# Stick-breaking attention weights from two sigmoids and a running product, longest rows first

## What is computed

```python
for i in range(s_len // 128):                       # rows lo..hi of the queries
    z = einsum('bthd,bshd->bhts', q[:, lo:hi], k[:, :hi]) * 64 ** -0.5
    mask = (lo + arange(128))[:, None] > arange(hi)[None, :]
    log_keep = where(mask, log_sigmoid(-z), 0.0)
    after = cumsum(log_keep, axis=3, reverse=True) - log_keep
    log_a = where(mask, log_sigmoid(z) + after, -inf)
    outs.append(einsum('bhts,bshd->bthd', exp(log_a), v[:, :hi]))
y = (o * silu(z_gate)) @ out_w
```

## Time and profile before

| | us |
|---|---|
| median of 3 runs | 1669.52 |
| profiled execution | 1669.38 |
| its span | 1667.6 |
| TensorE busy | 1577.1 (95%) |
| VectorE busy | 965.4 (58%) |
| ScalarE busy | 712.1 (43%) |

### The profile page before, as it was taken

The page is one execution under the profiler, slowest core; times in us unless marked ns, Lnnn a source line. Parts: engine busy times, 40 slices in busy tenths (PEclk is TensorE's granted clock), DMA queues, the critical chain, the costliest instruction groups (busy, mean ns, idle before and its releaser), DMA issues. The chain is left out here.

```text
span 1667.6 us, 19671 instructions
## 1 busy us (share of the span) xinstructions
PE 1577.1 (95%) x7998; PEld 1246.6 (75%) x7998; DVE 965.4 (58%) x1202; ACT 712.1 (43%) x997; POOL 112.1 (7%) x77
## 2 busy tenths in 40 slices
PE   6999999889899899889999999999999999999998
PEld 3777777667689665568787786668787888878877
DVE  3669888796774677755347626654444444432353
ACT  4555666563432567754212354532332222232241
POOL 0000000023200000004000000000020000000120
PEclk7999999999999999999999999999999999999999
DMA  7434333323572110102221112112222222232243
GB/s 306 154 128 152 126 130 136 138 64 152 202 303 102 51 51 29 48 33 106 93 75 46 58 51 90 66 73 87 90 76 101 101 93 86 100 113 89 97 155 114
DMA packets 47386, 177.76 MB, mean 107 GB/s; under 512 B 3616, under 2 KB 20256, under 8 KB 31680
## 3 DMA queue, kind: packets, MB, share of 16 engines
q1 hardware_dynamic: 30368, 167.44, 27.2%
q10 hardware_dynamic: 16928, 9.06, 2.1%
HBM read 172.23 MB, written 4.26 MB: 106 GB/s over the span
## 5 line engine op out<-in xcount | busy, mean ns | idle before, releaser
L636 PE MATMUL bank<-HH,whi 128*128 128x512 f32 x1352 | 560.7, 415 | 26.2 <-issue 10.3
L638 PE MATMUL bank<-HH,wlo 128*128 128x512 f32 x1352 | 533.4, 395 | 0.0
L637 PE MATMUL bank<-HL,whi 128*128 128x512 f32 x1352 | 533.4, 395 | 0.0
L636 PEld LDWEIGHTS bank<-HH,whi 128*128 128x128 f32 x1352 | 257.6, 191 | 112.2 <-issue 57.6
L1138 DVE TENSOR_TENSOR wlo<-raw,whi 128x2048 fp32r<-128x2048 f32 (+2 forms) x118 | 267.3, 2265 | 88.4 <-ACT whi L1805 84.9
L638 PEld LDWEIGHTS bank<-HH,wlo 128*128 128x128 f32 x1352 | 257.4, 190 | 55.9
L637 PEld LDWEIGHTS bank<-HL,whi 128*128 128x128 f32 x1352 | 258.1, 191 | 48.2 <-issue 3.1
L1805 ACT ACTIVATE whi<-raw 128x2048 fp32r<-128x2048 f32 (+2 forms) x118 | 222.3, 1884 | 117.0 <-PE bank L638 116.0
L2354 POOL TENSOR_TENSOR SR<-SR,tmp 128x512 f32<-128x512 f32 x30 | 55.1, 1835 | 614.5 <-ACT tmp L1822 613.6
L666 PE MATMUL bank<-whi,HH 128*128 128x256 f32 x256 | 74.3, 290 | 0.0
L667 PE MATMUL bank<-whi,HL 128*128 128x256 f32 x256 | 72.4, 283 | 0.0
(11 more groups left out here) (312 smaller groups left out, 2235.2 us busy)
## 6 DMA issues: line engine op xcount, KB each, us to landing
raw<-wstream SPq DMA_DIRECT2D x113, 1024.0 KB, 4.8
aslot<-tstream SPq DMA_DIRECT2D x24, 512.0 KB, 3.3
A<-astream SPq DMA_DIRECT2D x8, 1024.0 KB, 18.2
AC<-scratch ACTq DMA_DIRECT2D x16, 512.0 KB, 5.9
QT<-tstream SPq DMA_DIRECT2D x12, 512.0 KB, 5.2
OZ<-tstream SPq DMA_DIRECT2D x12, 512.0 KB, 7.4
raw<-wstream SPq DMA_DIRECT2D x4, 768.0 KB, 4.2
X<-xT SPq DMA_DIRECT2D x1, 2048.0 KB, 8.2
```

What stands on the lines that cost most here:

```text
L636: e.matmul(o, wh[:, k, c], hi[:, kb0 + k, :], start=first and k == 0, stop=False)
L637: e.matmul(o, wh[:, k, c], lo[:, kb0 + k, :], start=False, stop=False)
L638: x = e.matmul(o, wl[:, k, c], hi[:, kb0 + k, :], start=False, stop=last and k == kb - 1)
```

## The change

The scores are no longer clamped and masked. ScalarE reads `zz` twice and writes sigmoid(-z) into `keeps` and sigmoid(z) into `att`. VectorE scans `keeps` in place from the last column to the second: state = state x keep + diag. `diag` is 0 except for a unit matrix in the last 128 columns, so the state is 0 beyond the diagonal, becomes 1 on it, and is the running product after it. The weights are `att` times `keeps` shifted by one column; the column behind the last is set to 0 once. There is no exponential or logarithm left. Rounds hold fewer steps (37 rounds in place of 38, transposes of row r-2 and products of row r-3 in round r), `zz` is freed by `s_bk` from ScalarE, and a pair of heads begins with its row of four key blocks. ScalarE loads the sigmoid's table once before the `k` projection and the Exp and Ln table after the attention; the eight loads around Tanh are taken out. The diff, without the list of semaphore names and a renamed wait:

```diff
@@ -78,7 +78,7 @@
...
        ("m_norm_g", 16), ("kv_ada_b", 16), ("kv_norm_g", 8), ("final_g", 8), ("mix_g", 8),
        ("lb", 4), ("onorm", 1), ("qn", 1), ("kn", 1), ("ffn_g", 8), ("ple_g", 8), ("dtb", 1), ("alog", 1)]
-CON = [("ident", 128), ("ones", 128), ("bones", 128), ("cmask", 128), ("bmask", 512)]
+CON = [("ident", 128), ("ones", 128), ("bones", 128), ("cmask", 128), ("diag", 512)]
 
 
...
@@ -314,7 +314,7 @@
...
     ccol = lambda name: cc[:, COFF[name][0]:COFF[name][0] + COFF[name][1]]
     ident, ones, bones = ccol("ident"), ccol("ones"), ccol("bones")
-    cmask, bmask = ccol("cmask"), ccol("bmask")
+    cmask, diag = ccol("cmask"), ccol("diag")
     one = lambda name, k: cv[:, VOFF[name][0] + k:VOFF[name][0] + k + 1]
     eps_ap, eps2_ap = eps[:, 0:1], eps[:, 1:2]
...
@@ -430,8 +429,12 @@
...
 
 
-    att = lambda a, hi: W[:, 2 * (a % 5):2 * (a % 5) + 2, 0:hi]
-    att_z = lambda a, hi: (W[:, 10:12, 0:hi], W[:, 12:14, 0:hi], SR[:, :, 0:hi])[a % 3]
+
+    rows_of = lambda a: 3 - a % 4
+    width = lambda a: 128 * (rows_of(a) + 1)
+    att = lambda a, hi: W[:, 2 * (a % 4):2 * (a % 4) + 2, 0:hi]
+    keeps = flat(W[:, 8:14, :])[:, 0:4 * (S + 1)].rearrange("p (a s) -> p a s", a=4)
+    keep = lambda a, c0, c1: keeps[:, 2 * (a % 2):2 * (a % 2) + 2, c0:c1]
     live = lambda *units: [a for a in units if 0 <= a < 32]
 
...
@@ -826,21 +829,21 @@
...
 
         def attention():
-            for r in range(-1, 37):
-                for a in live(r - 4):
-                    w.wait_ge(s_ax, a + 1)
+            for r in range(-1, 36):
+                for a in live(r - 2):
+                    w.wait_ge(s_ls, a + 1)
                     w.wait_ge(s_at, a)
                     for j in range(2):
-                        for b in range(a % 4 + 1):
+                        for b in range(rows_of(a) + 1):
                             c = slice(128 * b, 128 * b + 128)
                             x = e.transpose(tt[:, j, c], att(a, S)[:, j, c], ident)
                     x.then_inc(s_tr, 1)
                 yield
-                for a in live(r - 5):
-                    n, tb = divmod(a, 4)
+                for a in live(r - 3):
+                    n, tb = a // 4, rows_of(a)
                     w.wait_ge(s_at, a + 1)
                     w.wait_ge(s_vt, 8)
-                    if tb == 0:
+                    if a % 4 == 0:
                         w.wait_ge(s_o, n)
                     for b in range(tb + 1):
...
@@ -850,14 +853,13 @@
...
                 yield
                 for a in live(r + 1):
-                    n, tb = divmod(a, 4)
-                    hi = 128 * (tb + 1)
+                    n, hi = a // 4, width(a)
                     w.wait_ge(s_qt, n + 1)
                     w.wait_ge(s_kt, n + 1)
-                    w.wait_ge(s_zc, a)
+                    w.wait_ge(s_bk, a)
                     for j in range(2):
                         o = 64 * j
-                        x = e.matmul(zz[:, j, 0:hi], QT[o:o + 64, n, 128 * tb:hi], KT[o:o + 64, n, 0:hi],
+                        x = e.matmul(zz[:, j, 0:hi], QT[o:o + 64, n, hi - 128:hi], KT[o:o + 64, n, 0:hi],
                                      start=True, stop=True)
                     x.then_inc(s_qk, 1)
...
@@ -866,7 +868,7 @@
...
         next(proj)
         so_first = both("so", 0, "so")
-        weave((attention(), 114), (chain(proj, take(so_first, 6)), 120))
+        weave((attention(), 111), (chain(proj, take(so_first, 6)), 120))
         run(so_first)
         for n in range(2, 8):
...
@@ -1426,37 +1428,29 @@
...
 
         def attention():
-            for r in range(-1, 37):
-                for a in live(r):
-                    hi = 128 * (a % 4 + 1)
-                    w.wait_ge(s_qk, a + 1)
-                    w.wait_ge(s_ls, a - 2)
-
-                    e.scalar_tensor_tensor(att_z(a, hi), zz[:, :, 0:hi], 40.0,
-                                           bmask[:, S - hi:S].unsqueeze(1).to_broadcast([128, 2, hi]),
-                                           ALU.min, ALU.add).then_inc(s_zc, 1)
-                yield
-                for a in live(r - 2):
-                    hi = 128 * (a % 4 + 1)
-                    av = att(a, hi)
-                    w.wait_ge(s_ex, a + 1)
+
+            own(e.memset(keeps[:, :, S:S + 1], 0.0))
+            for r in range(-1, 36):
+                for a in live(r - 1):
+                    last = slice(S - 1, S - width(a), -1)
+                    w.wait_ge(s_bk, a + 1)
                     for j in range(2):
-                        x = e.tensor_tensor_scan(av[:, j, ::-1], ones[:, 0:1].to_broadcast([128, hi]), av[:, j, ::-1], 0.0,
-                                                 ALU.mult, ALU.add)
+                        k = keep(a, 0, S)[:, j, last]
+                        x = e.tensor_tensor_scan(k, k, diag[:, last], 0.0, ALU.mult, ALU.add)
                     x.then_inc(s_sc, 1)
                 yield
-                for a in live(r - 2):
-                    hi = 128 * (a % 4 + 1)
-                    av = att(a, hi)
+                for a in live(r - 1):
+                    hi = width(a)
                     w.wait_ge(s_sc, a + 1)
-                    e.tensor_tensor(av, att_z(a, hi), av, ALU.subtract).then_inc(s_ls, 1)
+                    e.tensor_tensor(att(a, hi), att(a, hi), keep(a, S - hi + 1, S + 1), ALU.mult).then_inc(s_ls, 1)
+                yield
                 yield
 
...
         next(proj)
         e.tensor_tensor(G1[:, 24:32], vcol("final_g"), vcol("mix_g"), ALU.mult).then_inc(s_gain, 1)
-        weave((attention(), 114), (proj, 120))
+        weave((attention(), 111), (proj, 120))
         gate_att(7, aux[4][:, :])
         low("so", 6, OZ[:, 6, :])
...
@@ -1815,6 +1809,9 @@
...
             e.preload_act_table_set("natural_log_exp_and_others")
 
+        def sigmoids():
+            e.preload_act_table_set("sigmoid_and_others")
+
         def exptanh():
             e.preload_act_table_set("exp_and_others")
...
@@ -2004,6 +2001,7 @@
...
         for k in range(8):
             high_shifted("kv", k, ada[:, 24:32])
+        sigmoids()
         for n in range(8):
             if n % 2 == 0:
...
@@ -2046,12 +2044,10 @@
...
                 behind("sz", 2 * i4)
                 yield from idle(15)
-                exptanh()
                 for n in (2 * i4, 2 * i4 + 1):
                     w.wait_ge(s_blk, blk_done("sz", n))
                     w.wait_ge(s_sz, n - 2)
                     e.activation(T[n % 3][:, :], bank_of("sz", n)[:, :], ACT.Tanh, scale=0.5).then_inc(s_szt, 1)
-                lnexp()
                 if i4 > 0:
                     for n in (2 * i4 - 2, 2 * i4 - 1):
...
@@ -2062,36 +2058,33 @@
...
 
         def attention():
-            for r in range(-1, 37):
-                for a in live(r - 6):
+            for r in range(-1, 36):
+                for a in live(r):
+                    hi = width(a)
+                    w.wait_ge(s_qk, a + 1)
+                    w.wait_ge(s_ls, a - 1)
+                    w.wait_ge(s_av, a - 3)
+                    e.activation(keep(a, S - hi, S), zz[:, :, 0:hi], ACT.Sigmoid, scale=-1.0)
+                    e.activation(att(a, hi), zz[:, :, 0:hi], ACT.Sigmoid).then_inc(s_bk, 1)
+                yield
+                for a in live(r - 2):
+                    hi = width(a)
+                    w.wait_ge(s_tr, a + 1)
+                    e.activation(att(a, hi), tt[:, :, 0:hi], ACT.Copy).then_inc(s_at, 1)
+                yield
+                for a in live(r - 3):
                     if a % 4 == 3 and a < 31:
                         w.wait_ge(s_av, a + 1)
                         e.activation(QT[:, a // 4, :], aux[4][:, :], ACT.Copy).then_inc(s_o, 1)
-                for a in live(r - 3):
-                    av = att(a, 128 * (a % 4 + 1))
-                    w.wait_ge(s_ls, a + 1)
-                    e.activation(av, av, ACT.Exp).then_inc(s_ax, 1)
-                yield
-                for a in live(r - 1):
-                    hi = 128 * (a % 4 + 1)
-                    av = att(a, hi)
-                    w.wait_ge(s_zc, a + 1)
-                    w.wait_ge(s_av, a - 4)
-                    own(e.activation(av, att_z(a, hi), ACT.Exp))
-                    e.activation(av, av, ACT.Ln, bias=1.0).then_inc(s_ex, 1)
-                yield
-                for a in live(r - 4):
-                    hi = 128 * (a % 4 + 1)
-                    w.wait_ge(s_tr, a + 1)
-                    e.activation(att(a, hi), tt[:, :, 0:hi], ACT.Copy).then_inc(s_at, 1)
                 yield
 
...
         next(proj)
         next(proj)
-        weave((attention(), 114), (proj, 120))
+        weave((attention(), 111), (proj, 120))
         so_high(6)
         so_high(7)
+        lnexp()
         w.wait_ge(s_sum, SUM_AT["out"])
         w.wait_ge(s_gain, 7)
...
@@ -2445,8 +2438,8 @@
...
     bones = ((s // 64) == (t // 64)).astype(np.float32)
     cmask = (s <= t).astype(np.float32)
```

(9 more changed lines are left out.)

## The result

The changed kernel takes 1647.76 us (median of 4 runs, 1642.62 to 1651.21) where the kernel before takes 1669.40 (4 runs, 1667.16 to 1670.95): ratio 0.9869, 95% interval 0.9838 to 0.9899. It is faster by 21.6 us; 16.4 were forecast, and the time lies 0.7 us under the range. The profiled executions are 1669.4 and 1645.9 us, 23.5 apart (span 1644.0 after).

A forecast was written before the change was run, and what follows sets the result against it. TensorE's own work bounds the stage, apart from waits on overloaded ScalarE and VectorE and clock lost after them. Terms -21.7 + 4.5 + 0.8 = -16.4 us take 1669.4 to 1653.0, range 1648.5 to 1663.

The forecast's parts named there:

- ceiling: Stage from 557.5 to about 745.5 us: TensorE's waits, 14.9, plus lost clock, 6.8; at most 21.7 us to gain there.
- (c): Rival: Tanh drags its own table set in, so the loads stay; 1668 us, chance 0.06.
- (d): Rival: the two-operand scan takes 1.5 for 1.2 us, 5 us more; 1658 us; chance 0.25 shared with (a).
- (a): Rival: clusters at sz ends stay long, 12.6 us of waits and clock for 2.2; 1663; chance 0.25 shared with (d).
- (b): Rival: ScalarE holds zz too long, eight places at 3.6 us, 28.8 for 3.4; 1678 us; chance 0.09.
- The new waits: Local TensorE waits, mostly at block ends: 3.4 us summed plus 1.1 for steps not timed, 4.5 us.
- s = 96: sz block end at projection step 96: transposes wait 1.0 us for VectorE's multiplication, done at T + 4.3, wanted T + 3.4.
- s = 80: sz block end at projection step 80: TensorE waits 1.2 us for zz, freed at T + 5.9, wanted T + 4.8.
- four windows: Stretches after long waits, three of 10 us at clock 0.83, one of 12 at 0.86: 6.8 us lost.
- 1648.5: Floor of the forecast time in us: 1669.4 less the ceiling of 21.7, plus 0.8.
- `sigmoids()` before the chunk of `k`: Added table load delays the chunk and wlo, wanted by TensorE at 463.65: a new wait of 0.8 us (0.6 to 1.0).
- 20.5 us at the `sz` ends: TensorE's five rounds in the sz part; ScalarE's 21.4 and VectorE's 22.4 us exceed it before, 15 and 18.4 fit after.

The follow-up runs named there:

- e4: Changed kernel with an idle VectorE pass and an idle ScalarE copy per row and the eight table loads around Tanh back; 1657.9 us, ratio 0.993 to before.
- e10: Changed kernel with the eight table loads, the idle VectorE pass, and a ScalarE copy that the transposes wait for; 1659.8 us, ratio 0.995 to before.
- e7: Changed kernel with the shortest row of each pair of heads first; 1646.8 us, ratio 0.988 to before.
- e11: Changed kernel with 38 rounds and 114 attention steps again, as before; 1649.2 us, ratio 0.988 to before.
- e9: Changed kernel with one ScalarE copy per row in place, between VectorE's multiplication and the transposes, which wait for it; 1651.0 us, ratio 0.990 to before.
- e12: The changed kernel run once more, nothing altered; 1643.0 us, ratio 0.985 to before.
- e2: Changed kernel with one VectorE pass per row of the removed clamp's size, its result unused; 1650.4 us, ratio 0.988 to before.
- e6: Kernel before without its eight table loads, the gate's Tanh replaced by an exponential; 1662.4 us, ratio 0.996 to before.
- e1: Changed kernel with the eight table loads around Tanh back; 1655.6 us, ratio 0.990 to before.

## Why the prediction missed

**What held.** The ceiling's parts: TensorE's waits at the transposes, for `OZ` and for `SH` went, and the share of clock lost after them went too (clock 1.00 where 0.83 to 0.86 stood). The loads around Tanh are gone, and the only one left in the stretch is the added one at 719.12 us: Tanh and the sigmoids ran from one table set, as the Trainium skill (ScalarE: Activation LUTs; Table sets: the hidden batching unit) has it, so rival (c) is out. Rival (d) is out by the 1209 ns scan; the Trainium skill (DVE: opcode table, instruction layouts, handler registers and perf-mode slots; Datapath and trigger behaviour) names the fed-back result as what halves the rate, and the second operand did come free. Rivals (a) and (b) didn't happen: no score product is listed with a wait for `zz`, only three weight loads ahead of one, with 1.1 us in sum. Both removed clusters measured as the forecast had them, 25.7 and 33.2 us of busy time.

**What failed**, between the profiled executions, 23.5 us for 16.4:

1. *The new waits, 4.5 us: 0.9 measured.* This is the largest mis-sized term. The kernel after idles 3.35 us in the stretch, and 2.49 of them are the old wait behind the pair: 0.9 us are new. The ceiling had also left out a wait of 0.5 us at a score product, which went too. So idle time fell by 14.5 us where -14.9 + 4.5 = -10.4 were forecast. Of the places named, one came: s = 96, forecast 1.0, measured 0.7 (695.02 us, for line 1445). The one at s = 80, 1.2 us for `zz`, did not. TensorE in the kernel after, around that block end:

```profile
668.45 1.13 PE L862 MATMUL zz<-KT,QT 64*128 64x512 f32 x4
669.51 0.50 PE L639 MATMUL bank<-HH,whi 128*128 128x512 f32 x1
...
670.31 0.40 PE L639 MATMUL bank<-HH,whi 128*128 128x512 f32 x1
...
673.93 0.92 PE L862 MATMUL zz<-KT,QT 64*128 64x384 f32 x4
```

and ScalarE beside it:

```profile
668.56 0.60 ACT L2050 ACTIVATE tmp<-bank 128x512 f32<-128x512 f32 x1 [1.32 <-PE bank L641]
...
672.80 1.02 ACT L2068 ACTIVATE W<-zz 128x1024 f32<-128x1024 f32 x1
```

The block ends at T = 668.5. ScalarE frees `zz` at 673.8, T + 5.3 where T + 5.9 was forecast: Tanh takes 0.60, and each activation starts some 0.1 us before the recorded end of the one ahead. TensorE wants it at 673.9, T + 5.4 where T + 4.8 was forecast: two projection steps (669.51 and 670.31) stand between the score product and the transposes, and I had counted one. Twice 0.6 us is all there is between a wait of 1.2 and none. The 1.1 us I added for what I could not time pointed the wrong way as well.

2. *The clock after the wait of 2.49 us: 1.7 us left out.* The forecast kept that wait, and rightly, but it took over its clock loss with it without saying so: the ceiling counted only four windows. The forecast's stage ends ahead of the wait, and nothing is said of the clock behind it. In the kernel before it is 0.79:

```profile
748.00:756.00 8.00, 7.78 (x27) 6.26 (x28) 1.83 (x4) 3.66 (x4) 2.57 (x2) 0.79 0.36 131
```

8 x 0.21 = 1.7 us; in the kernel after, behind the same wait, it is 1.00 (the window from 727 us above). Over the whole stretch the clock gave back 8.6 us for 6.8 forecast. So 1648.5 was no floor. Nothing in the change acts on that wait, and in other kernels here the clock fell at it and in others not (last section), so these 1.7 us are not shown to be the change's work: they may be luck.

3. *`sigmoids()` before the chunk of `k`: 0.8 forecast, 0.27 measured.* The load, 459.08 to 460.36, moved `whi` and `wlo` as forecast (the latter to 462.40 to 464.69). But 463.65 is a product still on the old chunk; the first one on the new chunk comes one block later, in the kernel after at 464.79:

```profile
464.29 0.39 PE L641 MATMUL bank<-HH,wlo 128*128 128x512 f32 x1
464.79 0.47 PE L639 MATMUL bank<-HH,whi 128*128 128x512 f32 x1
```

It starts 0.50 us after its forerunner, where most products there start 0.23 us apart. The forecast had TensorE 0.9 us too early and `wlo` 0.4 too early.

Sum: 4.1 + 1.8 + 0.5 = 6.4 of the 7.1 us missed. The 0.7 left is spread over the rest of the program, and no row shows it apart. By the medians (21.6 us) the miss is 5.2, and the chosen measure moves it: the kernel after's own two sets of runs differ by 4.8 us.

**Where the gain comes from.** At 2.4 GHz the stage gained 14.7 us. The extra work alone, put back beside the chain, accounts for 6.5 (e4: loads 3.6, the VectorE pass 1.8, the ScalarE pass 0.6 singly). Putting the ScalarE pass into the chain makes that 11.1 (e10). About 1.8 is the order of the rows (e7) and 3.2 the meeting of steps (e11), which overlap with these and can't be added to them. The forecast argued from busy time against 20.5 us at the `sz` ends. That arithmetic fits the loads, but a pass's place in the chain counted for more than its busy time. The rest of the 23.2 us, about 8.5, is clock: four of its five falls stood behind waits that are gone (6.8 us), the fifth behind the wait that stayed (1.7).

**What stays open.** No run parts the number of handovers from the length of the chain: a pass added in the chain on the engine that holds the row already would. The rows of e10 speak for the handover, those of e9 for both. The 3.6 us between e10 and before: `zz` freed by VectorE rather than ScalarE, three buffers for the clamped scores, and a fourth handover differ there, and no run parts them. The clock of later stages differs between runs of one kernel, and no run tells why.

## What to carry to other kernels

Follow a tile's way from engine to engine and ask at each handover what that engine has queued, not only how busy each engine is: some 20 us of ScalarE work cost 0.6 us beside the chain and 4.5 in it. A wait forecast to a few tenths from an interleaving of two sequences is a coin toss (e11, 3.2 us for three steps), so it should widen the range in both directions and not shift its middle. When waits of TensorE go, look at the clock behind all of them, also behind the ones that stay, since it may or may not come back; and compare such kernels by span times granted clock.

## What the runs showed of the hardware

The granted clock of one and the same program ranged from 0.979 to 0.991 over ten runs, and its span from 1633.7 to 1649.4 us. Span times clock moved 5 us over six of them (e12) and 10 us over all ten. The same wait of 2.49 us at the pair's end stands in 13 traces here. In eight (before, e2 to e6, e9, e11) the clock fell at it, in five (after, e1, e7, e10, e12) it did not. So the length of a wait does not settle whether the clock falls; what does is left open here.

A table load cost ScalarE its own 1.28 us here and next to nothing beside it. The kernel after at the end of the stage:

```profile
719.12 1.28 ACT L1810 ACT_TABLE_LOAD   x1
720.42 1.92 ACT L1799 ACTIVATE whi<-raw 128x2048 fp32r<-128x2048 f32 x1
```

The next activation starts 1.30 us after the load. The Trainium skill (ScalarE: Activation LUTs; What ACT_TABLE_LOAD costs) adds a drain of 1.38 us; this trace shows none.
